# Rings of four for split weights, and the last two units of an output stage multiplied bank by bank

## The reference

```python
h = x
# first block
h = h + 0.5 * swiglu(rmsnorm(h, ffn1_norm), w_gate, w_up, w_down)          # width 2816
u = rmsnorm(h, mix_norm)
parts = split(u @ w_in)      # three attentions (forgetting, top-k sparse, memory) and gates
h = h + sum(gates * (branches @ w_branch)) @ w_out
h = h + 0.5 * swiglu(rmsnorm(h, ffn2_norm), ...)
# second block
xn = rmsnorm_2(h, g_mix)
z = xn @ w_in_2 + b_in_2                                  # a, gate, p
y = concatenate([conformer_conv(a, gate), multiscale_pool(p)])
h = h + y @ w_out_2
h = h + swiglu_2(rmsnorm_2(h, g_ffn), ...)
out = rmsnorm_2(h, g_final)
```

## Time and profile before

| | |
|---|---|
| median of 3 runs | 1861.6 us (1861.29 to 1863.54) |
| the profiled execution | 1862.35 us, its span 1860.5 us |
| mean granted clock of PE | 0.992 |
| busy: PE, PEld, DVE, ACT, POOL | 1794.2, 1434.9, 849.8, 637.5, 807.3 us |
| the same as share of the span | 96%, 77%, 46%, 34%, 43% |
| weights_low (L401) on POOL | 296 instructions, 2466 ns each |
| weights_high (L908) on ACT | 296 instructions, 1052 ns each |

### The profile page before, as it was taken

The page is one execution under the profiler, slowest core; times in us unless marked ns, Lnnn a source line. Parts: engine busy times, 40 slices in busy tenths (PEclk is TensorE's granted clock), DMA queues, the critical chain, the costliest instruction groups (busy, mean ns, idle before and its releaser), DMA issues.

```text
span 1860.5 us, 23214 instructions
## 1 busy us (share of the span) xinstructions
PE 1794.2 (96%) x8458; PEld 1434.9 (77%) x8458; DVE 849.8 (46%) x1207; ACT 637.5 (34%) x980; POOL 807.3 (43%) x355
## 2 busy tenths in 40 slices
PE   7999999999989998999999999999998999999997
PEld 5888888867777766787878888888765788888885
DVE  4333340077777898557543333300675443333003
ACT  5232321263232444565343232312423432323212
POOL 4444444454444522333454444444532544444443
PEclk9999999999999999999999999999999999999998
DMA  5232232322333211112322232322251222323221
GB/s 177 91 101 92 99 100 93 128 76 93 113 111 119 68 58 46 47 46 69 102 82 99 90 101 90 101 93 99 85 147 46 80 91 90 101 91 101 96 96 57
DMA packets 51070, 170.58 MB, mean 92 GB/s; under 512 B 6584, under 2 KB 7096, under 8 KB 50880
## 3 DMA queue, kind: packets, MB, share of 16 engines
q1 hardware_dynamic: 46368, 161.86, 26.5%
q10 hardware_dynamic: 4640, 7.89, 1.4%
HBM read 161.84 MB, written 2.11 MB: 88 GB/s over the span
## 4 chain that ended last, share of the span: by engine, by line
PE 61%; issue 15%; DVE 12%; POOL 8%; ACT 2%; DMA 1%; ACTq 0%; POOLq 0%; DVEq 0%; SPq 0%
PE bank L464 17%; PE bank L466 17%; PE bank L465 17%; POOL weights_low L401 7%; PE bank L646 4%; DVE top_keys L1445 2%; DVE top L1444 1%; PE bank L691 1%; DVE input_low L1242 1%; PE bank L810 1%; DVE head_root L1381 1%; PE bank L717 1%; DVE top_keys L1486 1%; DVE tile L1473 1%; PE bank L589 1%
## 5 line engine op out<-in xcount | busy, mean ns | idle before, releaser
L401 POOL TENSOR_TENSOR weights_low<-raw_weights,weights_high 128x1024 fp32r<-128x1024 f32 x296 | 729.7, 2466 | 1032.8 <-ACT weights_high L908 1032.8
L908 ACT CAST weights_high<-raw_weights 128x1024 fp32r<-128x1024 f32 x296 | 311.5, 1052 | 954.6 <-PE bank L466 884.4
L464 PE MATMUL bank<-input_high,weights_high 128*128 128x512 f32 x1488 | 592.1, 398 | 26.6 <-DVE input_low L1242 20.1
L466 PE MATMUL bank<-input_low,weights_high 128*128 128x512 f32 x1488 | 582.3, 391 | 0.0
L465 PE MATMUL bank<-input_high,weights_low 128*128 128x512 f32 x1488 | 581.9, 391 | 0.0
L464 PEld LDWEIGHTS bank<-input_high,weights_high 128*128 128x128 f32 x1488 | 281.3, 189 | 103.1 <-DVE input_low L1242 22.3
L465 PEld LDWEIGHTS bank<-input_high,weights_low 128*128 128x128 f32 x1488 | 281.3, 189 | 59.4 <-issue 2.6
L466 PEld LDWEIGHTS bank<-input_low,weights_high 128*128 128x128 f32 x1488 | 280.9, 189 | 59.4
L464 PE MATMUL bank<-hidden_high,weights_high 128*128 (+1 forms) x528 | 205.4, 389 | 0.0
L465 PE MATMUL bank<-hidden_high,weights_low 128*128 (+1 forms) x528 | 205.4, 389 | 0.0
L466 PE MATMUL bank<-hidden_low,weights_high 128*128 (+1 forms) x528 | 205.4, 389 | 0.0
(11 more groups left out here) (220 smaller groups left out, 1695.5 us busy)
## 6 DMA issues: line engine op xcount, KB each, us to landing
raw_weights<-weights SPq DMA_DIRECT2D x296, 512.0 KB, 3.4
tile<-tile ACTq DMA_DIRECT2D x36, 64.0 KB, 2.3
residual<-x_t SPq DMA_DIRECT2D x4, 512.0 KB, 7.7
out_t<-out_t SPq DMA_DIRECT2D x8, 256.0 KB, 2.2
glu_stacked<-glu_padded SPq DMA_DIRECT2D x24, 64.0 KB, 3.5
glu_stacked<-glu_padded ACTq DMA_DIRECT2D x24, 64.0 KB, 3.5
mem_in<-mem_t ACTq DMA_DIRECT2D x1, 1024.0 KB, 6.1
tile<-forget_sums ACTq DMA_DIRECT2D x4, 256.0 KB, 3.3
```

Of the source, the lines that this page charges most:

```text
L401: pool.tensor_tensor(wl[:, u % SPL, :], raw[:, u % RAW, :], wh[:, u % SPL, :].bitcast(F32), ALU.subtract).then_inc(low_done, 1)
L464: pe.matmul(out, wh[:, u % SPL, w], rh, start=start, stop=False)
L466: return pe.matmul(out, wh[:, u % SPL, w], rl, start=False, stop=stop)
L908: act.copy(wh[:, u % SPL, :], raw[:, u % RAW, :]).then_inc(high_done, 1)
```

## The change

Three things are done together.

1. `weights_low` no longer has memory of its own: it is laid over `raw_weights`, so POOL overwrites the raw unit in its slot with its low part. The memory that this frees goes to `weights_high`, and all three are rings of four (`RING`). The cast of unit u now waits for the end of unit u-4, and SP's transfer of unit u for the end of unit u-4 as well. ACT still casts two units ahead (`LEAD = 2`) at the same places of its queue, except in `feed`, where the cast comes before chunk 0 instead of before chunk 3. In `take_gates` the cast had waited for the end of the unit before the gate was copied; this wait is now written out. The copies into `glu_stacked` are issued one unit earlier in SP's order.
2. The last two units of each output stage are multiplied together (`spread_last`): for each bank first the last-but-one unit's block, then the last one's, and the bank is reported complete.
3. The high and low parts of `mixed` get tensors of their own (`wo2_high`, `wo2_low_pool`, `wo2_low`) instead of `input_high` and `input_low`.

```diff
@@ memory
-        raw = at("raw_weights", [P, RAW, DK * P], F32)
-        wh = at("weights_high", [P, SPL, DK * P], F32R)
-        wl = at("weights_low", [P, SPL, DK * P], F32R)
+        raw_at = base[0]
+        raw = at("raw_weights", [P, RING, DK * P], F32)
+        wl = at("weights_low", [P, RING, DK * P], F32R, raw_at)
+        wh = at("weights_high", [P, RING, DK * P], F32R)
...
+        wo2_high = at("wo2_high", [P, DK, S], F32R, big)
+        wo2_low_pool = at("wo2_low_pool", [P, 4, S], F32R, big + 8 * K2)
+        wo2_low = at("wo2_low", [P, 4, S], F32R, big + 22 * K2)
@@ SP
-                sp.wait_ge(low_done, u - RAW + 1)
-                sp.dma_start(raw[:, u % RAW, :], T["weights"][u]).then_inc(raw_loaded[u % RAW], 16)
+                sp.wait_ge(unit_done, u - RING + 1)
+                sp.dma_start(raw[:, u % RING, :], T["weights"][u]).then_inc(raw_loaded[u % RING], 16)
                 for c in STACKED:
-                    if u == U_IN2 + 2 * c + 7:
+                    if u == U_IN2 + 2 * c + 6:
@@ PE
+            def spread_last(name, u, first, second):
+
+                pe.wait_ge(low_done, u + 2)
+                for m in range(DK):
+                    mm = products(bank[m][:, :], u, m, *first, False, False)
+                    if m == DK - 1:
+                        mm.then_inc(unit_done, 1)
+                    mm = products(bank[m][:, :], u + 1, m, *second, False, True)
+                    mm.then_inc(sem(f"{name}_gathered") if m < DK - 1 else unit_done, 1)
...
-                for f in range(FC - 4, FC):
-                    spread_unit(name, u0 + f, hh[:, f, :], hl[:, f, :], u0 + f + 1, last=(f == FC - 1))
+                for f in range(FC - 4, FC - 2):
+                    spread_unit(u0 + f, hh[:, f, :], hl[:, f, :], u0 + f + 1)
+                spread_last(name, u0 + FC - 2, (hh[:, FC - 2, :], hl[:, FC - 2, :]), (hh[:, FC - 1, :], hl[:, FC - 1, :]))
@@ ACT
-                act.wait_ge(raw_loaded[u % RAW], 16 * trip if i is None else i * 16 + 16 * trip)
-                if u >= SPL or i is not None:
-                    act.wait_ge(unit_done, wait(u - SPL + 1))
-                act.copy(wh[:, u % SPL, :], raw[:, u % RAW, :]).then_inc(high_done, 1)
+                act.wait_ge(raw_loaded[u % RING], 16 * trip if i is None else i * 16 + 16 * trip)
+                if u >= RING or i is not None:
+                    act.wait_ge(unit_done, wait(u - RING + 1))
+                act.copy(wh[:, u % RING, :], raw[:, u % RING, :]).then_inc(high_done, 1)
...
             def feed(name, gain, u_last):
 
+                after(u_last)
                 for m in range(DK):
-                    if m == 3:
-                        after(u_last)
...
                     after(gate_unit(g))
+                    act.wait_ge(unit_done, gate_unit(g) + 1)
                     act.copy(gate_slot(g), bank[g % 2][:, :]).then_inc(sem("gates_out"), 1)
```

More of the change, by code:

```diff
@@ L366, in _ @@
                 sp.dma_start(dst[:, :], T[src]).then_inc(sem("constants_loaded"), 16)
-            for u in range(2, RAW):
+            for u in range(2, RING):
                 sp.dma_start(raw[:, u, :], T["weights"][u]).then_inc(raw_loaded[u], 16)
@@ L474, in project, with spread_unit @@
                 mm.then_inc(unit_done, 1)
-            def spread_unit(name, u, rh, rl, low_at, first=(), last=False, held=(None,)):
+            def spread_unit(u, rh, rl, low_at, first=(), held=(None,)):
                 pe.wait_ge(low_done, low_at)
@@ L645, in gate_products @@
                             w = slice(k * P, (k + 1) * P)
-                            mm = pe.matmul(bank[g % 2][:, :], (wl if part == 1 else wh)[:, u % SPL, w],
+                            mm = pe.matmul(bank[g % 2][:, :], (wl if part == 1 else wh)[:, u % RING, w],
                                            (xl if part == 2 else xh)[:, k, :],
@@ L786, in _ @@
             pe.wait_ge(sem("branches_read"), DK - 1)
-            for f in range(N_WO):
+            for f in range(N_WO - 2):
                 pe.wait_ge(sem("merged_low"), f + 1)
-                spread_unit("wo", U_WO + f, mgh[:, f, :], mgl[:, f, :], U_WO + f + 1,
-                            first=(6, 7, 0, 1, 2, 3, 4, 5) if f == 0 else (), held=(3, "branches_read", DK),
-                            last=(f == N_WO - 1))
+                spread_unit(U_WO + f, mgh[:, f, :], mgl[:, f, :], U_WO + f + 1,
+                            first=(6, 7, 0, 1, 2, 3, 4, 5) if f == 0 else (), held=(3, "branches_read", DK))
+            pe.wait_ge(sem("merged_low"), DK)
+            spread_last("wo", U_WO + N_WO - 2, (mgh[:, DK - 2, :], mgl[:, DK - 2, :]), (mgh[:, DK - 1, :], mgl[:, DK - 1, :]))
             gate_up("g2", "ffn2", U_GU2)
@@ L885, in _ @@
             pool_half(DK + 5, 4 * DK)
-            for c in range(4):
+            for c in range(2):
                 pe.wait_ge(sem("mixed_low"), 4 + c + 1)
-                spread_unit("wo2", U_WO2 + 4 + c, xh[:, c, :], xl[:, c, :], U_WO2 + 4 + c + 1, last=(c == 3))
+                spread_unit(U_WO2 + 4 + c, wo2_high[:, c, :], wo2_low[:, c, :], U_WO2 + 4 + c + 1)
+            pe.wait_ge(sem("mixed_low"), DK)
+            spread_last("wo2", U_WO2 + 6, (wo2_high[:, 2, :], wo2_low[:, 2, :]), (wo2_high[:, 3, :], wo2_low[:, 3, :]))
             gate_up("g3", "ffn3", U_GU3)
```

60 lines of the change are left out of this document (29 added, 31 removed).

## The result

The changed kernel takes **1844.0 us** (median of 4 runs, 1842.86 to 1845.14) against 1861.4 (1860.83 to 1863.54) before: a ratio of 0.9902, 95% interval 0.989 to 0.9914. That is 17.5 us faster, where 22.9 were forecast. The profiled execution took 1844.07 us with a span of 1842.2, 18.3 less than the span before.

What follows compares the result with a forecast made beforehand. PE, busy 96% of the span, was taken as the bound, so only its waits could give gain. Terms 15.3 + 1.5 + 4 + 2 + 1 - 0.9 = 22.9 us led to 1839 us; own range 1834 to 1845, stated range 1830 to 1850.

Steps and rivals of the forecast that it cites:

- (a): Four output-stage boundaries: multiplying the last two units bank by bank gains 15.3 us of 17.3 lost (8 to 17.3).
- a shared bandwidth: Alternative to DVE and POOL taking turns: an overlapped input_low would take some 1.5 us; no chance given.
- The cover that the prediction named for the sums: Boundaries: weights_low may hold DVE's last add until 21.8, just hidden because PE comes to the sums at 22.2.
- (b): End of the kernel: POOL's adds done earlier, so DVE's three adds take 2.1 us, not 3.62; gain 1.5 (0.9 to 1.8).
- (c): Rings of four in the steady stretches: already covered 9 us deep, gain and loss 0; POOL overwriting its input also 0.
- (d): First mixing block's projections: earlier casts free L1359 from POOL, period 1 to 2 us shorter; gain 4 (0 to 8).
- (e): Second mixing block: two DVE instructions no longer held by POOL, gain 2 (0 to 4); attention stage +1 (-2 to +4).
- (f): Start: third cast no longer waits for PE, POOL's weights_low falls on DVE's last input_low; loss 0.9 (0 to 1.8).
- Rival A: DVE keeps the boundaries, held by POOL with chunks of 2 us and more; time 1850; chance 0.15.
- B: Rival: the chains of (d) and (e) open fully and nothing is left at the boundaries; time 1830; chance 0.10.
- C: Slower rival: ACT's early cast waits for a late weight transfer at each boundary, a loss from 9.1 us landing; chance 0.05.
- the signs of being right: Stretches 11 to 11.8 us, input_low wait under 12, early residual add and cast, shorter period, end adds about 2.1 us.

Runs made afterwards that it cites:

- e3: The changed kernel with ACT's early cast in feed put back behind chunk 2 (before chunk 3): 1840.4 us, ratio 0.9885.
- e1: The changed kernel with the pair undone (last two units of an output stage one after the other again), rings and early cast kept: 1846.8 us, ratio 0.9915.
- e7: The changed kernel with the pair undone and the feed's cast back behind chunk 2; rings of four and wo2's own space kept: 1858.6 us, ratio 0.9982.
- e2: The kernel before with only the pair and wo2's own space added; rings and the cast's place as before: 1911.0 us, ratio 1.0262.
- e4: The changed kernel with ACT's wait for PE put back ahead of two casts (first feed-forward part, first mixing block's projections): 1842.2 us, ratio 0.9889.
- e8: e5 with the cast of wo2's first unit moved behind the root of the layer norm: 1827.0 us, ratio 0.9812.
- e5: e3 with two casts moved ahead (before the sigmoids; before DMA issues in the second mixing block), plus e4's two waits: 1830.2 us, ratio 0.9829.

## Why the prediction was right, and where not

The total came out within the range, but partly by luck: the boundaries gave 3.9 us less than forecast, the two mixing blocks together about what was forecast, though from other places and with help from the clock, and the first stage cost more.

**(a) The boundaries: right in kind, 15.3 forecast, 11.4 measured, and put down to the wrong edit.** The step that failed is "after that, 1.7 us a chunk beside POOL's four adds". The row behind it had POOL's adds in one piece, with squares in stock; with the pair the chunks start early and there is no stock, so POOL waits for ACT, ACT for DVE, and DVE in turn for POOL. Two chunks at each boundary take 2.16 us, and input_low of chunk 4 ends 15.5 us after the pair's start where 14.5 was forecast and PE wants it at 14.2. The row of e3 shows the stock restored and 1.7 us a chunk. The larger mistake is one of attribution. I gave the gain to "the last two units bank by bank" and took the cast ahead of chunk 0 as a detail of its start. e1 shows that the early cast, which the rings allow, brings the boundaries to 12.08 us without the pair (e7: 14.75 with the late cast). e3 shows that with the pair its new place costs 1.4 us at each. The list was right that this cast holds the first input_low to 7.7; it was not asked what the same list would be with the cast at its old place.

The Trainium skill's rule in "SBUF — State Buffer", section "SBUF: two separate sides" (of a DVE instruction with two SBUF inputs and a GpSimd instruction that reads SBUF, the later one waits for the whole of the other) was weighed in the prediction against a shared bandwidth. The trace agrees with it once more: at the boundary after, one input_low is 0.74 us alone, and 1.18, 1.64 or 2.37 beside POOL, which is what was left of POOL's instruction when it started (0.63, 1.09 and 1.83) plus 0.54 or 0.55.

The cover that the prediction named for the sums held: weights_low at 387.42 came on top of DVE's last adds, which took 4.21 us, and PE did not wait for them.

**(b) The end: 1.5 forecast, 1.45 measured.** POOL's adds are done by then, and DVE's three take 0.68 and 1.42 us instead of 3.62:

```profile
1827.18 0.68 DVE L1275 TENSOR_TENSOR tile<-tile,tile 128x512 f32<-128x512 f32 x1
1828.03 1.42 DVE L1275 TENSOR_TENSOR tile<-tile,tile 128x512 f32<-128x512 f32 x2 [0.17 <-ACT tile L935]
```

**(c) The rings in the steady stretches: 0 forecast, 0 measured.** The first feed-forward part is the same to 0.01 us. The rings' own gain stands in (d) and (e): e7, without the pair and the early cast, is 3.5 us faster than before. It gains 4.4 and 2.1 us there and 1.7 at the boundaries, and loses 2.9 at the start (1.5 of that the first matmul, see (f)) and 1.7 in the third feed-forward part, which begins at the lower clock in this execution. POOL writing onto its own input is not slower:

```profile
L405 POOL TENSOR_TENSOR weights_low<-raw_weights,weights_high 128x1024 fp32r<-128x1024 f32 x296 | 715.0, 2418 | 1020.2 <-ACT weights_high L924 1020.1
```

The mean was 2466 ns before. The longest wait for weights_low, 2.2 us, stayed as said. What (c) missed is what the rings allow: e2 shows that without them the pair costs 49 us. The prediction costed the ring as an edit of its own, and never asked what the pair would do in a ring of two.

**(d) The first mixing block: 4 and 1 forecast, 4.35 measured, and that agreement is luck.** The period of the projections fell from 21.3 us to 20.1, as expected, by the short L1375 (0.74 us, L1359 before, 2.13). But up to the fourth period's sum of squares (556.68 before, 557.14 after) the block is 1.2 us longer than before, where 4 were to be gained, and the attention stage behind it is 5.6 us shorter, where 1 was forecast:

```profile
556.68:911.62 354.94, 341.64 (x1933) 258.53 (x1933) 267.88 (x570) 170.91 (x392) 129.57 (x64) 0.99 0.21 67
```

```profile
557.14:906.49 349.35, 339.55 (x1933) 257.38 (x1934) 262.48 (x570) 172.16 (x393) 130.26 (x65) 1.00 0.21 69
```

What the projections lose comes ahead of the periods. The head start of a cast set a weights_low on L1390, and PE stands for 2.68 us ahead of 431.59 (e4, without that weights_low, has 1.16 there). Behind that wait the clock falls too, which costs another 1.6 us (14 matmuls in the stretch, seven of them at 0.63 us):

```profile
431.59:436.35 4.76, 4.76 (x14) 3.77 (x15) 4.15 (x4) 2.84 (x5) 1.74 (x3) 0.64 0.00 0
```

"The next multiplications are held by POOL too, at new places" had said the wait, without a place. What the attention stage gains is mostly a wait of the kernel before that the prediction didn't list, at the end of the same chain, with 1.6 us at the lower clock behind it, and one of 1.13 us at 647.67; both waits are gone:

```profile
596.15 0.72 PE L691 MATMUL bank<-idx_k,idx_q 64*128 64x128 f32 x8 [2.15 <-DVE causal_mask_rounded L1479]
```

In e1 and e7 the first mixing block shrank by 4.5 and 4.4 us, with the same pattern: this gain needs neither the pair nor the cast's new place.

**(e) The second mixing block: 2 forecast, 3.51 measured.** The 1.18 us wait is gone and the wait for the layer norm fell from 4.95 to 3.84. That is 2.3 us, by the mechanism named. The rest is the clock: in the six us behind the layer norm's wait it was 0.52 before and 0.72 after, and the way from there to the next part's first matmul is 1.1 us shorter.

```profile
1434.61:1440.61 6.00, 6.00 (x19) 5.08 (x20) 0.18 (x1) 0.26 (x1) 0.00 (x0) 0.52 0.24 82
```

```profile
1421.52:1427.52 6.00, 6.00 (x23) 4.95 (x24) 0.18 (x1) 2.48 (x3) 2.37 (x1) 0.72 0.00 0
```

The traces of e1, e3, e4 and e7, with the same code in this block, take 139.1 to 140.3 us for it, 0.9 to 2.1 less than before; in three of them the clock also fell behind the 2.16 us wait for weights_low. So the gain is 1 to 2 us, and the 3.51 are those of a favourable execution.

**(f) The start: -0.9 forecast, -2.36 measured, of which -1.39 are this term.** From first matmul to the sums: 16.33 us before, 17.72 after, within the 0 to 1.8 stated. POOL's weights_low stands on the last input_low as said; the second row is all six from the third on, and its end at 24.17 is that of the last, held to 0.55 us behind POOL's end:

```profile
20.90 2.72 POOL L405 TENSOR_TENSOR weights_low<-raw_weights,weights_high 128x1024 fp32r<-128x1024 f32 x1
...
12.27 11.90 DVE L1258 SCALAR_TENSOR_TENSOR input_low<-residual,vectors,input_high 128x512 fp32r<-128x512 f32 x6 [1.33 <-ACT input_high L934]
```

The other 0.97 us are the first matmul, at 10.05 instead of 9.08. Over the traces of this case it stands between 9.08 and 10.56, also in kernels that are alike up to there; ACT's first input_high waits for the landing of x_t, and starts at 7.34 before and 8.30 after. It isn't the change's.

Rival A (chunks above 2 us, 1850) had part of the mechanism: two chunks of each boundary. B's full boundaries came true only with e3. C's late transfer did not come: the cast's wait for its DMA ended 3.7 us after the pair's start. Of the signs of being right, two failed: the stretches of 11 to 11.8 us, and the wait on input_low under 12. It is 16.5, and would be over 12 with nothing left at the boundaries, for the first stage alone has 13.1 where the prediction counted 9.1. The others held: the first residual add 9.3 us before PE goes over, the cast's end, the period and the end's adds.

## What to carry to other kernels

When two edits aim at the same stall, write the list of who holds whom for each of them alone as well as for both: here each cured it, and together they were worse than one with the other's old place. A double pass over the last operands holds two slots of their ring until it ends: here a ring of two was too short and a ring of four enough (three wasn't tried). Check what each engine's queue waits for while these slots are occupied. Where an in-order engine prepares data for a second one that shares memory access with a third, the place of that preparation in the queue is worth moving, one instruction at a time: four such moves and two waits, none of which changes what is computed, brought 17 us here in the medians, as much as the change itself, though a part of it may be the clock's. And compare stretch by stretch before you call a sum right: term (d) came out at its forecast by a loss and a larger gain, neither of them where it was said.

## What the runs showed that was not expected

**A faster way through the attention part, behind a delay.** In the profiled execution of e8 the attention part of the first mixing block took 6.6 us less than in e5, with the same code there: 502.5 us against 509.1 from the first block's root spread to wo's first matmul. PE's waits for the normalised scores, in e5 and then in e8:

```profile
PE bank L721 <- DVE tile L1499: 5.5, 9, 1.4
```

```profile
PE bank L721 <- DVE tile L1499: 1.0, 2, 0.8
```

Up to 651 us both traces run alike. Then the granted clock of e8 falls to the lower level for a moment (0.57 over 4 us), for no wait that the profile shows longer than in e5, and PE loses 1.3 us:

```profile
651.50:655.50 4.00, 4.00 (x22) 2.76 (x20) 3.79 (x15) 1.73 (x6) 0.00 (x0) 0.57 0.00 0
```

From there on most of these waits are gone. So in this one execution the part ran 6.6 us shorter; by their times (1826.9 to 1828.1) the other three executions of e8 did not, which no trace shows. That the delay is the cause is not shown: a wait put in on purpose was not tried.

**The clock falls behind some waits and not behind others of the same length**: at one instruction it fell behind 2.15 us (e3) and not behind 2.16 (the changed kernel), at another behind 2.68 us (the changed kernel) and not behind 2.71 (e3). Each of these falls cost some 1.5 us. It may be a good part of the spread between executions of one kernel, which one trace of each can't show.
